# Expert weights through one ring of ten 2 MB pieces, and late blocks ahead of the expert's own up-projection

## The chip, the cores and the metric

One Trainium2 chip (trn2), one core of it. The time is that of the whole program on the device in microseconds (us); lower is better. All arithmetic is in float32.

## What is computed

One inference step of a hybrid decoder layer for 320 tokens (256 of a prompt, 64 of a sample group). The front of the layer (RMSNorm, an input projection, a convolution branch, a gated delta rule and a merge) is not touched by the change. What matters is the mixture of experts behind it:

```python
N_EXPERTS = 32; TOP_K = 4; D_MODEL = D_FF = 1024
logits = (h @ router_w) + router_b                    # 320 tokens
top_logit, top_idx = lax.top_k(logits, TOP_K)
gate = softmax(top_logit)
# for every expert e and the tokens that chose it:
gu = xe @ w_gate_up[e] + b_gate_up[e]                 # 1024 x 2048
gt, up = split(gu)
act = (clip(up, -7, 7) + 1) * (min(gt, 7) * sigmoid(1.702 * gt))
y = act @ w_down[e] + b_down[e]                       # 1024 x 1024
x = x + sum over the 4 experts of gate * y
```

The weights of one expert are 8 MB (gate and up) and 4 MB (down), 12 MB in all, and all 32 experts are read from HBM.

## The kernel before

The experts are computed one after the other. Each expert has 64 slots for its tokens (`SLOTS`). A token beyond the 64th goes into a **late block** of 32 slots (`LATE`); there can be up to 8 of them for an expert (`LATER`), and a table `flags` in SBUF, computed at run time from the routing, says which are needed. Every engine reads it with `value_load` and branches with `If`. In the data used here two of the 32 experts (numbers 10 and 30) need one late block each: the groups of the trace on 32 slots have twice the count of one block, and the two places are visible in time.

**The weights.** SBUF holds two buffers of 8 MB (`gu[0]`, `gu[1]`) for gate and up, used by even and odd experts in turn, and one buffer of 4 MB (`dn`) for the down weights. SyncE (SP) loads them in 2 MB transfers, four for a `gu` and two for a `dn`, each with its own semaphore. `released(e)` waits until the last down matmul of expert e is done (`y_mm`, and `late_y_mm` where the expert has late blocks), and then SP issues six transfers in a row: `dn` for expert e+1 and `gu` for expert e+2.

**TensorE (PE)**, in this order for each expert e: `up` (the bias, line 1007, then 32 matmuls against `gu`, line 1012), `gather` of the tokens of expert e+1 (line 986), for even e the `combine` of the pair before (line 1030), `turn_x` (line 994), the transposes of the activation (line 1088), `down` (16 matmuls against `dn`, line 1023). Most matmuls of the loop are 64 columns wide and go in pairs to two halves of the array. Where an expert has a late block, `late_up` is run ahead of the expert's own `down`, and `late_down` behind it, so that VectorE and ScalarE work on the late activation (`clamp`, the sigmoid, `swiglu`) while PE runs its own `down`. A further loop, `Fori(1, LATER)`, is entered only if a second late block is flagged.

**VectorE (DVE)** places the tokens of the next expert (line 1471), clamps and multiplies (lines 1495 to 1503), and adds the results to the residual (line 1510). **ScalarE (ACT)** does the sigmoid and the copies out of PSUM (lines 602 to 615).

PE, DVE, ACT and SP each run their own loop of 16 turns, two experts a turn, tied together by semaphores only. The code of both late variants (the straight one and the one in `Fori`) lies in the loop body, and is jumped over where it isn't needed.

Of the kernel before, what the change touches and what calls it, by code (L numbers as in the profile page):

```python
# [25 lines left out]
E = 32  # L26
SLOTS = 64
# [76 lines left out]
def hybrid_step(nc, xT, x_prompt, x_sample, w_main, w_ab, params, consts, conv_state, short_state,  # L104
# [3 lines left out]
    with ExitStack() as ctx:  # L108
# [91 lines left out]
        f[0] = gu_at[0] + 6 * 2 * D  # L200
# [54 lines left out]
        fg = region(KD * 2 * D, D)  # L255
        yout = region(KD * 2 * D + D, NT, D)
# [38 lines left out]
        def _(sp):  # L295
# [38 lines left out]
            def load_gu(e, p, parts=range(KD // 2)):  # L334
                for r in parts:
                    sp.dma_start(gu[p][:, 2 * r:2 * r + 2], w_gate_up[bass.ds(e, 1), 2 * r * P:2 * (r + 1) * P, :]
                                 .rearrange("o (k p) n -> p (o k) n", p=P)).then_inc(sem(f"ld_gu{p}_{r}"), 16)

            def load_dn(e):
                for r in range(2):  # L340
                    sp.dma_start(dn[:, 4 * r:4 * r + 4], w_down[bass.ds(e, 1), 4 * r * P:4 * (r + 1) * P, :]
                                 .rearrange("o (k p) n -> p (o k) n", p=P)).then_inc(sem(f"ld_dn{r}"), 16)


# [4 lines left out]
            load_gu(0, 0, (0, 1, 2))  # L349
# [3 lines left out]
            load_dn(0)  # L353
            load_gu(1, 1, (1,))
# [5 lines left out]
            load_gu(1, 1, (0,))  # L360

            sp.wait_ge(sem(FRONT_STORES[-1][0]), FRONT_STORES[-1][1])
            load_gu(0, 0, (3,))
# [3 lines left out]
            load_gu(1, 1, (2, 3))  # L367
            blocks = sp.alloc_register("sp_blocks")
            sp.reg_mov(blocks, 0)

            def released(e):

                sp.wait_ge(sem("y_mm"), e + 1)
                later = sp.value_load(flags[0:1, bass.ds(e * LATER, 1)], min_val=0, max_val=1)
                with sp.If(later):
                    sp.reg_add(blocks, blocks, 1)
                    more = sp.value_load(flags[0:1, bass.ds(e * LATER + 1, 1)], min_val=0, max_val=1)
                    with sp.If(more):
                        with sp.Fori(1, LATER) as b:
                            f = sp.value_load(flags[0:1, bass.ds(e * LATER + b, 1)], min_val=0, max_val=1)  # L380
                            with sp.If(f):
                                sp.reg_add(blocks, blocks, 1)
# [57 lines left out]
        def _(act):  # L440
# [157 lines left out]
            with expert_loop(act, 0, E // 2) as i:  # L598
                for p in range(2):
                    e = 2 * i + p  # L600
                    act.wait_ge(sem("clamped"), e + 1)
                    act.activation(actb, tmp, ACT.Sigmoid, scale=ALPHA).then_inc(sem("sig"), 1)  # L602
                    act.wait_ge(sem("x_gathered"), e + 2)
                    act.wait_ge(sem("xg_mm"), e + 1)
                    act.activation(xt, ps[:, 3, :], ACT.Copy).then_inc(sem("xt_ready"), 1)  # L605
                    act.wait_ge(sem("t_mm"), e + 1)
                    act.activation(actT, heads(0, P, P), ACT.Copy).then_inc(sem("gt_ready"), 1)  # L607
                    if p:
                        act.activation(gT, ps[:, 1, 0:N], ACT.Copy).then_inc(sem("gt_ready"), 1)  # L609
                    later = act.value_load(flags[0:1, bass.ds(e * LATER, 1)], min_val=0, max_val=1)  # L610
                    with act.If(later):
                        late_up(act.snap(blocks))
                    act.wait_ge(sem("y_mm"), e + 1)
                    act.activation(ysb[SLOTS * p:SLOTS * (p + 1), 0], ps[0:SLOTS, 2, :], ACT.Copy)  # L614
                    act.activation(ysb[SLOTS * p:SLOTS * (p + 1), 1], ps[SLOTS:P, 2, :],
                                   ACT.Copy).then_inc(sem("y_ready"), 1)
                    with act.If(later):
                        late_down(act.snap(blocks))
                        act.reg_add(blocks, blocks, 1)
                        more = act.value_load(flags[0:1, bass.ds(e * LATER + 1, 1)], min_val=0, max_val=1)  # L620
                        with act.If(more):
                            with act.Fori(1, LATER) as b:
                                f = act.value_load(flags[0:1, bass.ds(e * LATER + b, 1)], min_val=0, max_val=1)
                                with act.If(f):
                                    m = act.snap(blocks)
                                    late_up(m)
                                    late_down(m)
                                    act.reg_add(blocks, blocks, 1)
# [9 lines left out]
        def _(pe):  # L638
# [365 lines left out]
            def up(slots, outs, tokens, s, w, waits, done):  # L1004
# [3 lines left out]
                for k in range(KD):  # L1008
                    if waits is not None and k % 2 == 0:
                        pe.wait_ge(waits[k // 2][0], waits[k // 2][1])  # L1010
                    for q in range(4):
                        m = pe.matmul(outs[q], tokens[:, k % 4, k // 4], w[:, k, q * 512:(q + 1) * 512],  # L1012
                                      start=False, stop=(k == KD - 1))
                m.then_inc(done, 1)

            def down(slots, arrived, ready, done, i):
                pe.wait_ge(ready, i)
                for k in range(KD):
                    if arrived is not None and k % 4 == 0:
                        pe.wait_ge(sem(f"ld_dn{k // 4}"), arrived)  # L1020
                    for c in range(2):
                        a = (k // 4) * slots
                        m = pe.matmul(ps[slots * c:slots * (c + 1), 2, :], actT[:, k % 4, a:a + slots],  # L1023
                                      dn[:, k, c * 512:(c + 1) * 512], start=(k == 0), stop=(k == KD - 1))
                m.then_inc(done, 1)
# [46 lines left out]
            with expert_loop(pe, 0, E // 2) as i:  # L1072
                for p in range(2):
# [13 lines left out]
                    for j in range(4):  # L1087
                        m = pe.transpose(ps[:, 0, j * P:(j + 1) * P], actb[:, j * P:(j + 1) * P], ident)  # L1088
# [573 lines left out]
```

## Time and profile before

| what | value |
|---|---|
| time, median of 3 runs | 1512.07 us (1510.52 to 1519.53) |
| time of the profiled execution | 1514.72 us |
| its span, first to last instruction | 1512.9 us |
| mean granted TensorE clock | 0.956 of full speed |
| PE busy | 1408.2 us (93%) |
| DVE busy, ACT busy | 490.8 us (32%), 216.8 us (14%) |
| moved by DMA | 444.70 MB, mean 294 GB/s |

The first 457 us are the front of the layer, then the expert loop runs to about 1496 us, then comes the end (two norms and the store). Matmuls are pipelined, so their durations overlap: the time that a series takes is read from its first start to the start of what follows. Granted clock 1.00 is 2.4 GHz, and 0.5 is 1.2 GHz.

### The profile page before, as it was taken

The page shows a single profiled execution, that of the slowest core. Times are in us where ns is not written, and L with a number is a line of the kernel's source. Part 1 is how long each engine was busy: PE and PEld are TensorE (multiplying, and loading weights), DVE is VectorE, ACT ScalarE, POOL GpSimd, SP SyncE. Part 2 cuts the span into 40 slices and gives each one's busy share as a digit, 9 for nine tenths or more (in the row PEclk, how much of TensorE's full clock was granted, in tenths as well). Part 3 has the DMA queues.
Part 4 walks back from the last instruction along what each step waited for, and adds up shares of the span by engine and source line. Part 5 has one row for each costly group of instructions (what it writes and reads, how often), then busy time and mean ns, then how long its engine had stood idle before and what let it go on. Part 6 is the DMA issues. An engine that isn't in the chain of part 4 may idle for free.

```text
span 1512.9 us, 17366 instructions
## 1 busy us (share of the span) xinstructions
PE 1408.2 (93%) x6338; PEld 661.5 (44%) x6339; DVE 490.8 (32%) x1237; ACT 216.8 (14%) x364; POOL 36.5 (2%) x44
## 2 busy tenths in 40 slices
PE   6997998998979899999999999999999999999996
PEld 4665766886433333333333333333333333333332
DVE  2596626433453122221322132122221222213223
ACT  2111252210110101111110111101111011111102
POOL 3101001000000000000000000000000000000000
PEclk9998998987968999999998999999999999999999
DMA  9748212014382999999993899999999999999941
GB/s 245 141 134 85 92 56 56 1 57 138 158 340 113 387 396 420 418 416 417 419 419 121 353 402 419 415 401 419 409 417 396 409 416 408 417 417 419 418 159 35
DMA packets 82924, 444.70 MB, mean 294 GB/s; under 512 B 6224, under 2 KB 7136, under 8 KB 50000
## 3 DMA queue, kind: packets, MB, share of 16 engines
q1 hardware_dynamic: 79600, 435.88, 74.2%
q0 software_dynamic: 2720, 7.13, 1.9%
q10 hardware_dynamic: 576, 1.31, 0.3%
q8 instruction: 18, 0.29, 0.1%
q14 instruction: 10, 0.08, 0.0%
HBM read 439.92 MB, written 4.39 MB: 294 GB/s over the span
## 4 chain that ended last, share of the span: by engine, by line
PE 90%; DMA 4%; DVE 2%; ACT 2%; issue 1%; ACTq 0%; DVEq 0%; SPq 0%
PE ps L1012 30%; PE ps L1023 16%; PE ps L669 9%; PE ps L986 7%; PE ps L1030 6%; PE ps L1007 4%; DMA arena<-in_w_main 2%; PE ps L887 2%; DMA arena<-in_b_gate_up 1%; PE ps L880 1%; PE ps L774 1%; PE ps L708 1%; PE ps L994 1%; PE ps L653 1%; PE ps L1088 1%
## 5 line engine op out<-in xcount | busy, mean ns | idle before, releaser
L1012 PE MATMUL ps<-arena 128*64 128x512 f32 (+1 forms) x2176 | 472.0, 595 | 0.0
L1012 PEld LDWEIGHTS ps<-arena 128*64 128x64 f32 (+1 forms) x2176 | 168.4, 136 | 290.7 <-issue 290.7
L1023 PE MATMUL ps<-arena 128*64 128x512 f32 (+1 forms) x1088 | 260.0, 611 | 19.1 <-ACT arena L609 17.5
L1495 DVE TENSOR_SCALAR arena<-ps 128x512 f32<-128x512 f32 (+1 forms) x34 | 23.6, 693 | 674.1 <-PE ps L1012 674.1
L669 PE MATMUL ps<-arena 128*128 128x320 f32 x576 | 162.0, 445 | 16.5 <-DMA arena<-in_w_main 10.9
L1023 PEld LDWEIGHTS ps<-arena 128*64 128x64 f32 (+1 forms) x1088 | 85.4, 139 | 167.9 <-issue 166.0
L669 PEld LDWEIGHTS ps<-arena 128*128 128x128 f32 x576 | 112.5, 196 | 65.6 <-issue 20.2
L986 PE MATMUL ps<-arena 128*64 128x512 f32 (+3 forms) x420 | 115.9, 617 | 8.9 <-DMA arena<-in_b_gate_up 5.0
L1030 PE MATMUL ps<-arena 128*128 128x512 f32 (+3 forms) x228 | 101.9, 606 | 3.8 <-ACT arena L592 1.4
L1510 DVE TENSOR_TENSOR arena<-arena,ps 128x512 f32<-128x512 f32 (+1 forms) x114 | 72.7, 680 | 61.8 <-PE ps L1030 61.8
L602 ACT ACTIVATE arena<-arena 128x512 f32<-128x512 f32 x32 | 20.2, 632 | 483.6 <-DVE arena L1495 483.6
L1007 PE MATMUL ps<-arena 128*64 128x512 f32 (+1 forms) x272 | 78.0, 633 | 3.7 <-issue 2.4
L986 PEld LDWEIGHTS ps<-arena 128*64 128x64 f32 (+3 forms) x420 | 30.4, 135 | 78.0 <-issue 72.4
L1030 PEld LDWEIGHTS ps<-arena 128*128 128x128 f32 (+3 forms) x228 | 34.1, 171 | 60.0 <-issue 53.3
L1182 DVE SCALAR_TENSOR_TENSOR arena<-arena 128x256 f32<-128x256 f32 x120 | 56.7, 472 | 0.0
L614 ACT ACTIVATE arena<-ps 64x512 f32<-64x512 f32 x32 | 18.9, 591 | 249.5 <-PE ps L1023 249.5
L1007 PEld LDWEIGHTS ps<-arena 128*64 128x64 f32 (+1 forms) x272 | 22.5, 139 | 41.9 <-issue 40.4
L1490 DVE TENSOR_TENSOR arena<-ps,arena 128x256 f32<-128x256 f32 (+1 forms) x70 | 26.0, 413 | 45.3 <-PE ps L994 33.3
L1185 DVE SCALAR_TENSOR_TENSOR arena<-arena 128x64 f32<-128x64 f32 x120 | 32.7, 272 | 0.0
L607 ACT ACTIVATE arena<-ps 128x512 f32<-128x512 f32 x32 | 19.2, 600 | 88.1 <-PE ps L1088 62.4
L994 PE MATMUL ps<-arena 128*128 128x128 f32 x132 | 21.2, 285 | 11.2 <-ACT arena L605 11.2
L1477 DVE TENSOR_SCALAR arena<-arena 128x64 f32<-128x64 f32 (+3 forms) x108 | 30.4, 311 | 1.3
(280 smaller groups left out, 1008.3 us busy)
## 6 DMA issues: line engine op xcount, KB each, us to landing
arena<-in_w_gate_up SPq DMA_DIRECT2D x128, 2048.0 KB, 24.1
arena<-in_w_down SPq DMA_DIRECT2D x64, 2048.0 KB, 12.4
arena<-in_w_main SPq DMA_DIRECT2D x40, 512.0 KB, 3.7
arena<-in_w_merge_out SPq DMA_DIRECT2D x1, 3072.0 KB, 10.2
arena<-in_w_conv_out POOLq DMA_DIRECT2D x1, 2048.0 KB, 14.2
arena<-in_w_delta_out SPq DMA_DIRECT2D x1, 2048.0 KB, 8.0
out_delta_s<-arena POOLq DMA_DIRECT2D x1, 2048.0 KB, 20.7
arena<-in_xT SPq DMA_DIRECT2D x1, 1280.0 KB, 6.4
```

The costliest lines, as they stand in the source:

```text
L669: i = pe.matmul(ps[:, j, 0:N], wring[:, j, k], hT[:, k], start=(k == 0), stop=(k == KD - 1))
L887: i = pe.matmul(ps[0:P, 2 * t + c, :], mixed[:, k, tok(t)], wm[k][:, c * 512:(c + 1) * 512], start=(k == 0), stop=(k == KD - 1))
L986: m = pe.matmul(ps[slots * c:slots * (c + 1), 3, :], pk[rows(t), t, 0:slots], h2_of(t)[:, c * 512:(c + 1) * 512], start=(t == 0), stop=(t ...
L994: return pe.transpose(out, rows_in, ident)
L1007: pe.matmul(outs[q], s[:, q, 0:slots], bg, start=True, stop=False)
L1012: m = pe.matmul(outs[q], tokens[:, k % 4, k // 4], w[:, k, q * 512:(q + 1) * 512], start=False, stop=(k == KD - 1))
L1023: m = pe.matmul(ps[slots * c:slots * (c + 1), 2, :], actT[:, k % 4, a:a + slots], dn[:, k, c * 512:(c + 1) * 512], start=(k == 0), stop=(k ...
L1030: m = pe.matmul(ps[0:TILES[t][1], COMBINE_BANKS[t][c], :], g(c)[:, tok(t)], y(c), start=True, stop=True)
L1182: stt(out=cacc[:, j, 0:NP], in0=cext[:, j, bass.ds(w, NP)], scalar=dw_w[:, j, bass.ds(w, 1)], in1=cacc[:, j, 0:NP], op0=ALU.mult, op1=ALU. ...
L1185: stt(out=seqs(cacc[:, j]), in0=cext_s[:, j, :, bass.ds(w, TS)], scalar=dw_w[:, j, bass.ds(w, 1)], in1=seqs(cacc[:, j]), op0=ALU.mult, op1 ...
L1477: i = ts(out(t), iot(rows(t)), pos[rows(t), t, bass.ds(e, 1)], gates[rows(t), t, bass.ds(e, 1)], ALU.is_equal, ALU.mult)
L1510: tt(part, part, ps[0:n, COMBINE_BANKS[t][c], :], ALU.add).then_inc(done, 1)
```

## The change

**The ring.** The same 20 MB of SBUF are cut into ten slots of 2 MB. An expert's weights are six pieces (four of gate and up, two of down), numbered through all experts; piece n goes into slot n mod 10. A new semaphore `used` counts pieces whose last matmul is done; SP waits for it before each piece, and each refill is one transfer, instead of six behind one wait. `released` and SP's reading of `flags` are gone.

**The loops.** Since six pieces and ten slots repeat only after five experts, and the parity of two experts is needed too, the loop bodies of PE, DVE and ACT now hold ten experts (`BODY`), three turns, and the last two experts are written out behind the loop. SP's loop holds thirty pieces, five turns.

**Late blocks.** `late_up` and `late_down` are joined to `late_block`, which runs at the head of the expert, ahead of its own `up`. All late blocks go through one `Fori(0, LATER)` with an `If` inside; it is entered if the first flag is set, and makes 8 turns. The flag of a second block is no longer asked for before the loop. DVE and ACT do the same in their own loops.

```diff
+BODY = 10
+RING_SLOTS, PER_EXPERT = 10, 6
+SLOT_AT = [16384, 20480, 24576, 28672, 32768, 36864, 4096, 0, 8192, 12288]
...
-        gu_at = [KD * 2 * D, 0]
-        gu = [region(at_, KD, 2 * D) for at_ in gu_at]
-        dn = region(2 * KD * 2 * D, KD, D)
+        gu_slot = [region(a, 2, 2 * D) for a in SLOT_AT]
+        dn_slot = [region(a, 4, D) for a in SLOT_AT]
...
+            def load(e, u, slot):
+
+                if u < 4:
+                    rows_in = w_gate_up[bass.ds(e, 1), 2 * u * P:2 * (u + 1) * P, :]
+                    out = gu_slot[slot]
+                else:
+                    rows_in = w_down[bass.ds(e, 1), 4 * (u - 4) * P:4 * (u - 3) * P, :]
+                    out = dn_slot[slot]
+                sp.dma_start(out, rows_in.rearrange("o (k p) n -> p (o k) n", p=P)).then_inc(sem(f"ld_ring{slot}"), 16)
...
-            load_gu(1, 1, (2, 3))
...
-            def released(e):
-
-                sp.wait_ge(sem("y_mm"), e + 1)
-                later = sp.value_load(flags[0:1, bass.ds(e * LATER, 1)], min_val=0, max_val=1)
-                with sp.If(later):
-                    sp.reg_add(blocks, blocks, 1)
...
-                    sp.wait_ge(sem("late_y_mm"), sp.snap(blocks))
-                    sp.sem_inc(sem("late_released"), 1)
...
-            with expert_loop(sp, 0, E // 2 - 1) as i:
-                for p in range(2):
-                    released(2 * i + p)
-                    load_dn(2 * i + (p + 1))
-                    load_gu(2 * i + (p + 2), p)
-            released(E - 2)
-            load_dn(E - 1)
+            load(1, 2, 8)
+            load(1, 3, 9)
...
+            def refill(first, n):
+
+                u = n % PER_EXPERT
+                sp.wait_ge(sem("used"), first * PER_EXPERT + (n + 1 - RING_SLOTS))
+                load(first + n // PER_EXPERT, u, n % RING_SLOTS)
+
+            for n in range(RING_SLOTS, 5 * PER_EXPERT):
+                refill(0, n)
+            with expert_loop(sp, 1, E // 5) as i:
+                for n in range(5 * PER_EXPERT):
+                    refill(5 * i, n)
+            for n in range(2 * PER_EXPERT):
+                refill(E - 2, n)
+            sp.wait_ge(sem("used"), (E - 2) * PER_EXPERT + 3)
...
+                act.wait_ge(sem("used"), PER_EXPERT * e + 6)
...
+            def arrived(laps, n, u):
+
+                g = n * PER_EXPERT + u
+                pe.wait_ge(sem(f"ld_ring{g % RING_SLOTS}"), laps + 16 * (g // RING_SLOTS + 1))
+                return g % RING_SLOTS
...
+                for u in range(4):
+                    w = gu_slot[arrived(laps, n, u)]
+                    for r in range(2):
+                        k = 2 * u + r
+                        for q in range(4):
+                            m = pe.matmul(outs[q], tokens[:, k % 4, k // 4], w[:, r, q * 512:(q + 1) * 512],
+                                          start=False, stop=(k == KD - 1))
+                    if slots == SLOTS:
+                        m.then_inc(sem("used"), 1)
+                    elif u == 3:
+                        m.then_inc(done, 1)
...
+                for u in range(4, 6):
+                    w = dn_slot[arrived(laps, n, u)]
...
+                    if slots == SLOTS:
+                        m.then_inc(sem("used"), 1)
...
+            def late_block(m, laps, n):
...
+                up(LATE, [ps[LATE * q:LATE * (q + 1), 0, :] for q in range(4)], late_xg, sel[n % 2],
+                   laps, n, sem("late_h_mm"))
...
+                down(LATE, laps, n, sem("late_gt_ready"), sem("late_y_mm"), m + 1)
...
-            with expert_loop(pe, 0, E // 2) as i:
-                for p in range(2):
...
-                    later = pe.value_load(flags[0:1, bass.ds(e * LATER, 1)], min_val=0, max_val=1)
-                    with pe.If(later):
-
-                        pe.wait_ge(sem("gt_ready"), down_ready)
-                        late_up(pe.snap(blocks), p)
-                    down(SLOTS, 16 * e + 16, sem("gt_ready"), sem("y_mm"), down_ready)
-                    with pe.If(later):
-                        late_down(pe.snap(blocks))
-                        pe.reg_add(blocks, blocks, 1)
-                        more = pe.value_load(flags[0:1, bass.ds(e * LATER + 1, 1)], min_val=0, max_val=1)
-                        with pe.If(more):
-                            with pe.Fori(1, LATER) as b:
-                                f = pe.value_load(flags[0:1, bass.ds(e * LATER + b, 1)], min_val=0, max_val=1)
-                                with pe.If(f):
-                                    m = pe.snap(blocks)
-                                    late_up(m, p)
-                                    late_down(m)
-                                    pe.reg_add(blocks, blocks, 1)
+            def expert(first, pairs, laps, n):
+
+                e, p, pair = first + n, n % 2, pairs + n // 2
+                pe.wait_ge(sem("xg_ready"), e + 1)
+                pe.wait_ge(sem("sel_ready"), e + 1)
+                later = pe.value_load(flags[0:1, bass.ds(e * LATER, 1)], min_val=0, max_val=1)
+                with pe.If(later):
+                    with pe.Fori(0, LATER) as b:
+                        f = pe.value_load(flags[0:1, bass.ds(e * LATER + b, 1)], min_val=0, max_val=1)
+                        with pe.If(f):
+                            late_block(pe.snap(blocks), laps, n)
+                            pe.reg_add(blocks, blocks, 1)
+                up(SLOTS, [ps[SLOTS * (q % 2):SLOTS * (q % 2 + 1), q // 2, :] for q in range(4)], xg[p], sel[p],
+                   laps, n, None)
+                gather(SLOTS, sem("p_ready"), sem("x_gathered"), e + 2)
...
+                down(SLOTS, laps, n, sem("gt_ready"), None, 3 * pair + (3 if p else 1))
+
+            with expert_loop(pe, 0, E // BODY) as i:
+                for n in range(BODY):
+                    expert(BODY * i, BODY // 2 * i, 16 * PER_EXPERT * BODY // RING_SLOTS * i, n)
+            for n in range(E % BODY):
+                first = E - E % BODY
+                expert(first, first // 2, 16 * PER_EXPERT * first // RING_SLOTS, n)
...
+            def clamp(n, gate, mm, count, clamped):
+                dve.wait_ge(mm, count)
```

**PE, the place of the late block.** Before, in the body for an even expert: behind the last combine (line 1030), the flag is read, and the late gather, turn and up (on 32 slots) stand ahead of `down` (line 1023).

```order
L1030 MATMUL ps<-arena 64x512 x2
L1099 ISA
L1099 TENSOR_LOAD arena
L1099 ISA x2
L1100 COMPARE_AND_BRANCH
L1102 ISA
L1103 ISA
L986 MATMUL ps<-arena 32x512 x6
L995 MATMUL ps<-arena 128x64 x4
L1007 MATMUL ps<-arena 32x512 x4
L1012 MATMUL ps<-arena 32x512 x32
```

Now, at the end of the late block (late down, line 1028, and combine, line 1038) and the head of the expert's own up (lines 1007 and 1013):

```order
L1028 MATMUL ps<-arena 32x512 x16
L1038 MATMUL ps<-arena 128x512 x4
L1062 ISA
L1038 MATMUL ps<-arena 64x512 x2
L1088 REGISTER_ALU
L1086 UNCONDITIONAL_BRANCH
L1084 REGISTER_ALU
L1084 COMPARE_AND_BRANCH
L1083 UNCONDITIONAL_BRANCH
L1007 MATMUL ps<-arena 64x512 x4
L1001 ISA
L1013 MATMUL ps<-arena 64x512 x32
```

The late block has moved from around the expert's own `down` to ahead of its own `up`, and the counter and back branch of the loop over late blocks (line 1084) stand between the two.

**PE, the head of the late block.** What is passed on the way from the flag to the first late matmul, for every expert; both COMPARE_AND_BRANCH rows can jump, the first over the whole block (lines 1083 to 1088), the second over one turn of it:

```order
L1082 ISA
L1082 TENSOR_LOAD arena
L1082 ISA x2
L1083 COMPARE_AND_BRANCH
L1084 UNCONDITIONAL_BRANCH
L1084 ISA
L1085 TENSOR_LOAD arena
L1085 ISA x2
L1086 COMPARE_AND_BRANCH
L1087 ISA
L980 MATMUL ps<-arena 32x512 x6
```

Each turn of the loop over late blocks, also one without a block, passes lines 1085, 1086 and 1084.

**SP, the refills.** Before, six transfers stand in a row behind one wait (lines 341 and 336; the row on line 374 belongs to the wait for the next expert):

```order
L341 DMA arena<-in_w_down 128x4x1024
L336 ISA
L336 DMA arena<-in_w_gate_up 128x2x2048
L336 ISA
L336 DMA arena<-in_w_gate_up 128x2x2048
L336 ISA
L336 DMA arena<-in_w_gate_up 128x2x2048
L336 ISA
L336 DMA arena<-in_w_gate_up 128x2x2048
L374 ISA
```

Now each transfer has its own wait (line 376, with a register), and there is no flag to read:

```order
L376 REGISTER_ALU
L344 ISA
L344 DMA arena<-in_w_down 128x4x1024
L376 REGISTER_ALU
L344 ISA
L344 DMA arena<-in_w_down 128x4x1024
L376 REGISTER_ALU
L344 ISA
L344 DMA arena<-in_w_gate_up 128x2x2048
```

## Rows read from the trace of the kernel before

**Rows 1.** The page, busy time by engine, and DMA in 40 slices.

```profile
PE 1408.2 (93%) x6338; PEld 661.5 (44%) x6339; DVE 490.8 (32%) x1237; ACT 216.8 (14%) x364; POOL 36.5 (2%) x44
...
DMA  9748212014382999999993899999999999999941
```

**Rows 2.** Windows: stretch, length, busy PE, PEld, DVE, ACT, POOL, clock, DMA, GB/s.

```profile
641.80:701.80 60.00, 58.21 (x267) 21.98 (x263) 14.23 (x32) 7.64 (x12) 0.00 (x0) 1.00 1.02 418
761.80:827.00 65.20, 59.82 (x285) 19.72 (x283) 16.41 (x35) 8.00 (x13) 0.00 (x0) 0.92 0.61 246
917.00:978.70 61.70, 59.91 (x265) 22.43 (x263) 14.24 (x32) 7.64 (x12) 0.00 (x0) 0.97 1.02 417
1163.40:1224.90 61.50, 59.71 (x267) 22.05 (x263) 14.24 (x32) 7.64 (x12) 0.00 (x0) 0.97 1.01 408
1404.80:1465.00 60.20, 54.97 (x285) 18.48 (x279) 15.58 (x34) 8.00 (x13) 0.00 (x0) 1.00 0.65 262
```

**Rows 3.** Waits, 457 to 1505 us: who waited for whom, us, times, longest.

```profile
PE ps L1023 <- ACT arena L609: 17.5, 16, 1.1
...
PE ps L994 <- ACT arena L605: 11.2, 16, 0.7
...
PE ps L986 <- DVE arena L1471: 3.9, 2, 1.9
```

**Rows 4.** DMA issues, 641 to 702 us: count, size, median us to landing.

```profile
arena<-in_w_gate_up SPq DMA_DIRECT2D x8, 2048.0 KB, 24.9
```

**Rows 5.** Chain of waits, whole loop: start, us, what (gathers at experts 8 to 11).

```profile
717.25 2.72 PE ps L986 x12
...
748.66 2.75 PE ps L986 x11
...
777.23 2.72 PE ps L986 x12
...
843.89 2.75 PE ps L986 x12
```

**Rows 6.** Chain of waits, 1404 to 1500 us: expert 30 with its late block.

```profile
1420.27 2.72 PE ps L986 x12
...
1431.31 2.92 PE ps L986 x12
...
1444.51 7.02 PE ps L1023 x32
1451.53 1.03 PE ps L995 x8
...
1465.34 1.94 PE ps L1007 x8
...
1481.01 2.75 PE ps L986 x12
```

**Rows 7.** Timeline of DVE, 1444 to 1448 us: the activation of that late block.

```profile
1444.58 0.68 DVE L1495 TENSOR_SCALAR arena<-ps 64x512 f32<-64x512 f32 x1 [6.42 <-PE ps L1012]
...
1447.40 0.68 DVE L1503 SCALAR_TENSOR_TENSOR arena<-arena 64x512 f32<-64x512 f32 x1
```

**Rows 8.** Sources of L1108, L1100 and L1105: PE's sequencer, ns min/median/max, starts.

```profile
L1108 PEldq TENSOR_LOAD <-arena x2: 312/314/315, 825.4 to 1464.3; - x2
...
L1100 PEldq COMPARE_BRANCH  x32: 83/223/340, 481.9 to 1485.6; - x32
...
L1105 PEldq COMPARE_BRANCH  x32: 67/227/5888, 486.4 to 1489.7; - x32
...
L1105 PEldq COMPARE_BRANCH  x2: 670/3279/5888, 486.4 to 515.0; - x2
```

**Rows 9.** Timeline of PE at 521 us, the first back edge.

```profile
521.64 0.65 PE L1007 MATMUL ps<-arena 128*64 128x512 f32 x2 [2.23 <-issue]
```

**Rows 10.** DMA queues, 457 to 522 us, then 522 to 1480 us: packets, MB, share.

```profile
q8 instruction: 6, 0.10, 0.6%
...
q1 hardware_dynamic: 63522, 370.70, 94.9%
```

More of the change, by code:

```diff
@@ L198, in hybrid_step @@
         unit = early(P)
-        f[0] = gu_at[0] + 6 * 2 * D
+        f[0] = SLOT_AT[3]
         s0 = early(NSEQ * H, P)
@@ L630, in _ @@
+            with expert_loop(act, 0, E // BODY) as i:
+                for n in range(BODY):
+                    expert(BODY * i, n)
+            for n in range(E % BODY):
+                expert(E - E % BODY, n)
             for t in range(NT):
@@ L1002, in turn_x, with up @@
                 m.then_inc(done, 1)
-            def up(slots, outs, tokens, s, w, waits, done):
+            def arrived(laps, n, u):
+                g = n * PER_EXPERT + u
+                pe.wait_ge(sem(f"ld_ring{g % RING_SLOTS}"), laps + 16 * (g // RING_SLOTS + 1))
+                return g % RING_SLOTS
+            def up(slots, outs, tokens, s, laps, n, done):
                 for q in range(4):
                     pe.matmul(outs[q], s[:, q, 0:slots], bg, start=True, stop=False)
[L1008 to L1014, printed above, removed]
@@ new lines, in down @@
+            def down(slots, laps, n, ready, done, i):
+                pe.wait_ge(ready, i)
+                for u in range(4, 6):
+                    w = dn_slot[arrived(laps, n, u)]
+                    for r in range(4):
+                        k = 4 * (u - 4) + r
+                        for c in range(2):
+                            a = (k // 4) * slots
+                            m = pe.matmul(ps[slots * c:slots * (c + 1), 2, :], actT[:, k % 4, a:a + slots],
+                                          w[:, r, c * 512:(c + 1) * 512], start=(k == 0), stop=(k == KD - 1))
+                    if slots == SLOTS:
+                        m.then_inc(sem("used"), 1)
+                    elif u == 5:
+                        m.then_inc(done, 1)
@@ L1122, in _ @@
+            combine(1, *halves, sem("c_mm"))
             pe.wait_ge(sem("added"), 3 * E + 2)
-            combine(2, *pair, sem("c_mm"))
+            combine(2, *halves, sem("c_mm"))
         @block.vector
@@ new lines, in expert @@
+            def expert(first, pairs, n):
+                e, p, pair = first + n, n % 2, pairs + n // 2
+                dve.wait_ge(sem("x_gathered"), e + 1)
+                later = dve.value_load(flags[0:1, bass.ds(e * LATER, 1)], min_val=0, max_val=1)
+                with dve.If(later):
+                    with dve.Fori(0, LATER) as b:
+                        f = dve.value_load(flags[0:1, bass.ds(e * LATER + b, 1)], min_val=0, max_val=1)
+                        with dve.If(f):
+                            late_block(e, lambda r: iota[r, bass.ds(b * LATE + SLOTS, LATE)], dve.snap(blocks))
+                            dve.reg_add(blocks, blocks, 1)
+                place(e + 1, first_slots, SLOTS, sem("p_ready"))
+                select(e + 1, 1 - p)
+                clamp(P, ps[:, 0, :], sem("used"), PER_EXPERT * e + 4, sem("clamped"))
+                weigh(e, lambda t: pg[rows(t), t, p], first_slots)
+                swiglu(P, ps[:, 1, :], sem("sig"), sem("act_ready"), sem("swiglu_step"), e)
+                if p == 0:
+                    add(0, sem("c_mm"), sem("added"), pair)
+                move_x(xg[1 - p], SLOTS, sem("xg_mm"), sem("xg_ready"), e + 2)
+                if p == 0:
+                    add(1, sem("c_mm"), sem("added"), pair)
+                    add(2, sem("c_mm"), sem("added"), pair)
@@ L1577, in final_norm @@
+            with expert_loop(dve, 0, E // BODY) as i:
+                for n in range(BODY):
+                    expert(BODY * i, BODY // 2 * i, n)
+            for n in range(E % BODY):
+                expert(E - E % BODY, (E - E % BODY) // 2, n)
             def final_norm(t):
```

190 lines of the change are left out of this document (60 added, 130 removed).

## The prediction

> **What bounds the kernel now.** I read the page first, for the engines; then windows of two experts each; then the list of waits; and the chain of waits for what stands between two gathers. PE is busy 93% of the span, and in the expert loop nearly always; but the DMA engines are full there too [rows 1]. So which of them sets the pace? An undisturbed pair of experts takes 60.0 us, 58.2 of them PE busy at full clock, while DMA moves at 418 GB/s [rows 2]. A pair's weights are 12 pieces of 2 MB (2.097 million bytes), 25.17 MB, which at 418 GB/s take 60.2 us. The two are level, within 0.2 us a pair. The list of waits decides: over the whole loop PE waits for ACT (17.5 and 11.2 us in 16 times, the small gaps of every odd expert) and for DVE ahead of a late block [rows 3]. No row of that list has PE or its weight loads waiting for a DMA. The weights are just in time (24.9 us from issue to landing, behind a queue of other pieces [rows 4]), but in time. The loop is bound by PE, and what is not paid for by PE's own matmuls is: the small ACT gaps, two late blocks, five pairs at a granted clock of 0.97 (from 917 to 1225 us, 61.5 to 61.7 us each; first and last in [rows 2]), and one stall of 2.2 us [rows 9].
>
> **The ring (refills piece by piece).** It removes SP's wait for the whole expert: the first refill can start when the first two k-rows of expert 0 are done, where before it had to wait for that expert's down; by the windows of an expert that is some 25 us earlier. It doesn't change bytes or the number of transfers (192 of 2 MB), so the DMA pace stays 60.2 us a pair. A PE that never waited for DMA can't gain from earlier pieces: worth 0. It costs 0 as well: the pieces are ahead by some 25 us at the start and lose 0.2 us a pair, 3 us in 16 pairs. The longest stretch without a release, a late block, finds the ring full behind it. In the two late pairs DMA share falls to 0.61 and 0.65 [rows 2], so DMA has slack there before and after. The waits per piece on PE are as many as before (six an expert), increments ride on matmuls, and SP's register adds lie in a queue that otherwise waits. If that cover were gone (a piece late by 1 us in each expert) it would be 32 us; nothing in the rows asks for it.
>
> **The late blocks.** First their price before. Gathers of consecutive experts stand 748.66 - 717.25 = 31.4 us apart from even to odd; with the late block of expert 10 it is 843.89 - 777.23 = 66.7 [rows 5], and with that of expert 30 it is 1481.01 - 1420.27 = 60.7 [rows 6]. So they cost 35.2 and 29.3 us. The 5.9 between them go with the clock: 0.92 in the first stretch, 1.00 in the second [rows 2].
> Now the same work ahead of the expert's own up, from the second. (a) Gather, turn and up: 1444.51 - 1431.31 = 13.2 us. The wait of 1.9 us for DVE ahead of them [rows 3] goes, since DVE has the tokens placed long before; it is not counted in the 13.2. (b) Then PE needs the activation. Before, the expert's own down (7.0 us, 1444.51 to 1451.53 [rows 6]) covered that; now nothing does. DVE starts 1444.58 and ends 1447.40 + 0.68 = 1448.08 [rows 7]: 3.6 us idle PE. (c) The turns, the late down and the combine: 1465.34 - 1451.53 = 13.8 us. Together 30.6 us.
> (d) The loop over late blocks now makes eight turns, seven of them empty. Each reads a flag and passes two branches and a register add. The row for it: the one check of a second block before, whose load starts at 1464.3 [rows 8], is over when up starts at 1465.34 [rows 6], so 1.0 us for load, assertion and branch; another branch is 0.22 [rows 8], with the add and the gaps of a load's neighbours I take 0.4 more. 1.4 x 7 = 9.8 us a late expert; bounds 1.0 x 7 = 7 and 1.6 x 7 = 11. PE has only the last combine queued, 1.1 us, to cover it, so 8.7 are seen. DVE and ACT make the same empty turns at the same time, not longer ones, and have the next clamp 14 us later.
> Sum: 30.6 + 8.7 = 39.3 us for a late expert against 29.3: +10.0 each. For expert 10 I let the clock cost what it cost before. For expert 30, PE now pauses 3.6 and 8.7 us where it paused not at all and the granted clock may fall: between 0 and the 5.9 that expert 10 shows; I take 3. **+23 us** for the late blocks.
>
> **The longer body.** Every expert without a late block (30) jumps over it once, about 310 instructions; and there are two back edges and a fall out of the loop. Before there were two such jumps an expert, of some 190 and 430, and sixteen turns. (A float32 matmul is two MATMULs and two weight loads in the trace; counted so in the listings, a body had some 1,770 instructions on PE before, and has some 5,800 now.) Of the jumps the trace shows: the branch on line 1105 takes 0.23 us as a rule, and once 5.9 us, in the first turn [rows 8]. PE stood still for 2.23 us after it [rows 9]. PE's queue thus covers 3.7 us of a slow branch. In that first turn 6 packets came on the instruction queue, and none from 522 to 1480 us [rows 10]: a body that has been loaded is run without loading. The body of ten experts is new in its first turn and, if what was loaded is only kept for a body of the old size, new in the other two as well. Bounds: 0 (loading goes on ahead, and jumps stay cheap, as both on line 1100 and one of two on line 1105 were in the first turn, 0.67 us at most [rows 8]), and 32 x 2.23 = 71 us (each jump and back edge like the slow one). The jump is nearer to the short one in length, and of the long ones one in two was cheap; I take three to four slow ones, at the back edges and where a jump lands far out, 4 x 2.23 = 8.9, less the one of before: **+7 us**.
> The Trainium skill speaks against this part of the change: "Runtime: NRT & Kernel Launch", section on instruction fetch, says that TensorE holds 2048 instructions, refilled in blocks of 256, that straight code is loaded ahead, and that a taken branch to a target outside what is held waits for a load. By its figures the old body fits and the new one doesn't (an estimate from that page), so it would have every turn of the new body load again; whether each jump then stalls is the rival below.
>
> **The clock.** The five pairs at 0.97 cost 1.5 to 1.7 us each, 8 in all. Where PE's gaps fall decides it, and these shift: between -8 and +8, and I take 0.
>
> **Sum.** The profiled execution took 1514.7 us, 2.6 over the median of the runs. 1514.7 + 23 + 7 = 1544.7, and on the scale of the median 1542.
>
> **Rivals.**
> *Code loading at each jump.* If each of the 30 jumps and 2 back edges is like the slow one, 1512 + 23 + 71 = 1606 us. For it: the page's rule, and that jumps over loaded code are the only ones that the steady state shows. Against: three of four jumps in the first turn were under 0.7 us. From 3.7 us on a branch is seen on PE at all, so single short loads would cost nothing. Chance 0.25, for all from ten slow jumps on (1560 and more).
> *No change.* The clock gives it back: PE's phase shifts, the five pairs run at 60.0 (-8), expert 10 escapes its half clock (-5.9), expert 30 keeps its full clock (-3), and no jump is slow (-7): 1542 - 24 = 1518 us. The point: granted clock 1.00 in all pairs. For it: 0.97 in only five of sixteen pairs, so it is a matter of phase. Against: PE now has longer pauses. Chance 0.17 for 1497 to 1527.
> *The ring is worth something.* If PE were paced by the weights after all, in ways that the list of waits doesn't tell, the slow pairs (8), the stall of 2.2 and the 5.9 of expert 10 could be such time, and go, with the late blocks' new gaps hidden in it: 1512 - 16 = 1496 us. For it: DMA at 418 GB/s as full as PE. Against: no wait for a DMA in the list, and the time lost lies where the granted clock is low. Chance 0.03.
> *The forecast,* 1527 to 1560: 0.55.
>
> **Range and chances.** About 1% (15 us) is what a measurement can tell from no change. The lower end reaches to the no-change case, 1519; the upper takes in the code loading up to 24 slow jumps, 1512 + 23 + 54 = 1589. Faster by over 1%: 0.03; within 1%: 0.17; slower: 0.80.
>
> **What would show it.** In the chain of waits after: pairs still 60.0 us; at experts 10 and 30 a PE gap of 3.6 us ahead of the late transposes, and one of 8 to 10 ahead of L1007, with no late wait for DVE; gather to gather 71 and 71 us in place of 66.7 and 60.7. Instruction packets on q8 all through the loop, some 70 more. The branch on line 1083 short in most experts, over 3.7 us in three or four. Refills landing well ahead of use. The forecast is wrong if the pair itself isn't 60.0, if that branch is long in most experts, or if the empty turns of the late loop cost much less or more than 1.4 us.

## The result and the profile after

The changed kernel takes 1563.11 us (median of 4 runs, 1559.92 to 1569.85), the kernel before 1515.36 us beside it: ratio **1.032 [1.029, 1.035]**. The profiled execution of after has a span of 1568.1 us, 55.2 more than before; it is the longest of the four runs (1569.85), so the rows show some 7 us more than the medians do.

The page: PE busy, the instruction queue, and the first matmuls of `up` with PE's idle time ahead of them.

```profile
PE 1430.1 (91%) x6338; PEld 660.2 (42%) x6339; DVE 491.8 (31%) x1237; ACT 202.8 (13%) x353; POOL 36.6 (2%) x44
...
q8 instruction: 86, 1.41, 0.4%
...
L1007 PE MATMUL ps<-arena 128*64 128x512 f32 (+1 forms) x272 | 87.7, 688 | 35.2 <-issue 34.0
```

As many matmuls as before (x6338), with 22 us more of busy time, and 34 us marked "issue": idle time of PE in which it waited for nothing that the profile shows.

Waits from 457 to 1565 us, and DMA issues from 457 to 1500 us.

```profile
PE ps L1007 <- issue: 34.0, 10, 9.3
...
PE ps L1028 <- ACT arena L612: 16.5, 16, 1.1
...
PE ps L988 <- ACT arena L608: 11.2, 16, 0.7
...
PE ps L989 <- DVE arena L1504: 7.3, 2, 3.6
```

```profile
arena<-in_w_gate_up SPq DMA_DIRECT2D x122, 2048.0 KB, 13.0
```

The small ACT gaps are those of [rows 3], the first of them 1 us less in all (16.5 for 17.5). The wait for DVE's place is gone, and the uncovered activation (L989 for L1504) has come, 3.6 us twice. The pieces land 13.0 us after their issue, where [rows 4] had 24.9 (24.5 over the whole loop): a single refill has fewer others ahead of it than one of six issued together. No row has PE waiting for a DMA, before or after.

The chain of waits from 757 to 880 us, expert 10 with its late block at the head (start, us, what).

```profile
757.96 2.75 PE ps L980 x11
...
778.45 1.94 PE ps L1007 x8
780.38 8.85 PE ps L1013 x64
...
795.23 10.03 PE ps L1028 x32
...
809.52 9.32 issue
818.84 3.33 PE ps L1007 x8
822.16 13.73 PE ps L1013 x64
835.89 2.72 PE ps L980 x12
```

Gather to gather (L980) is 835.89 - 757.96 = 77.9 us, and at expert 30 it is 77.9 again, where I had 71. The row of 9.32 us is the seven empty turns; VectorE stands 10.1 us in its own at the same time, and ScalarE 8.8. The late up takes 1.94 + 8.85 us and the late down 10.03. In the chain of before that [rows 6] is taken from, the same three are:

```profile
1436.58 1.07 PE ps L1007 x8
1437.64 6.87 PE ps L1012 x64
...
1453.86 7.08 PE ps L1023 x32
```

The windows of after tell why (stretch, length, busy PE, PEld, DVE, ACT, POOL, clock, DMA, GB/s):

```profile
777.30:784.10 6.80, 6.22 (x32) 1.76 (x34) 2.02 (x8) 0.50 (x1) 0.00 (x0) 0.50 0.64 266
784.10:794.40 10.30, 6.65 (x59) 2.41 (x51) 2.75 (x4) 0.63 (x1) 0.00 (x0) 1.00 0.01 2
794.40:801.20 6.80, 6.01 (x15) 1.30 (x16) 0.00 (x0) 0.70 (x2) 0.00 (x0) 0.50 0.00 0
801.20:811.40 10.20, 7.09 (x32) 1.78 (x28) 3.74 (x6) 0.59 (x1) 0.00 (x0) 1.00 0.00 0
811.40:821.70 10.30, 2.86 (x8) 1.05 (x10) 0.72 (x4) 1.28 (x1) 0.00 (x0) 0.50 0.00 0
```

The granted clock is 0.50 (1.2 GHz) in three stretches around the late block: 23.9 us. Around the same block before it was one of 10.2 and one of 3.4, and at expert 30 none. Each fall comes after a pause of PE: ahead of the late transposes of the tokens (1.2 us), of the activation (3.6 us), and in the empty turns. A fourth stretch of 3.4 us lies between the same two gathers, at 763.6 us, behind the small gap of 1.0 us ahead of the odd expert's down, and expert 30 has one too; before, the late pairs had none there. From 784 us on the DMA share is 0: all ten slots are full.

The branch on line 1083 over the late block (PE's sequencer; ns min/median/max), then its slowest, and a stall after a short one with PE's timeline.

```profile
L1083 PEldq COMPARE_BRANCH  x32: 71/360/6132, 457.9 to 1517.1; - x32
...
L1083 PEldq COMPARE_BRANCH  x1: 6132/6132/6132, 1312.1 to 1312.1; - x1
...
L1083 PEldq COMPARE_BRANCH  x1: 355/355/355, 876.9 to 876.9; - x1
```

```profile
880.25 0.59 PE L1007 MATMUL ps<-arena 128*64 128x512 f32 x1
883.11 1.12 PE L1007 MATMUL ps<-arena 128*64 128x512 f32 x2 [2.28 <-issue]
```

The branch is short in most experts and over 3.7 us in four (4.7 to 6.1); six more took 1.5 to 1.9 us, with no stall behind them. The chain shows 2.56, 1.35, 1.96 and 2.62 us of idle PE behind those four. It shows 2.18, 2.28 and 2.13 more behind branches of 0.35 us: at 883 us one matmul behind the jump ran, and the next came late. All stalls but the empty turns are 34.0 - 9.32 - 9.13 = 15.6 us, where before had 2.2.

**Where the 55.2 us are.** The time from DVE's clamp of one expert to that of the next (both experts of a pair) splits the loop. An undisturbed pair has 59.9 to 60.0 us in both kernels. The two pairs with late blocks took 184.5 us together before and 218.7 after: **+34.2**. The rest of the loop took 19.4 more: 13.4 of stalls, and eight pairs with a stretch of half clock instead of five, 1.6 us each, 4.8; 1.2 aren't placed. Three of the eight stretches begin in or within 1.1 us of a stall (those at 521, 645 and 881 us), the other five behind the small gap as before. Whether the stalls made them isn't shown: the kernel of old buffers and one turn below has no stall in its loop and eight such stretches too. The front took 1.7 more.

### The profile page after: what moved, and what is told of

Same layout as the page of the kernel before. It is cut to its first block, busy times and chain, and to the rows that moved or that the text cites. A ratio compares the mean times of both kernels' runs of the same rounds, so it can differ in the third digit from the quotient of the medians.

```text
span 1568.1 us, 17347 instructions
## 1 busy us (share of the span) xinstructions
PE 1430.1 (91%) x6338; PEld 660.2 (42%) x6339; DVE 491.8 (31%) x1237; ACT 202.8 (13%) x353; POOL 36.6 (2%) x44
## 4 chain that ended last, share of the span: by engine, by line
PE 89%; DMA 3%; issue 3%; DVE 2%; ACT 2%; ACTq 0%; DVEq 0%; SPq 0%
PE ps L1013 29%; PE ps L1028 16%; PE ps L663 9%; PE ps L980 6%; PE ps L1038 6%; PE ps L1007 4%; PE ps L881 2%; DMA arena<-in_w_main 2%; DMA arena<-in_b_gate_up 1%; PE ps L874 1%; PE ps L768 1%; PE ps L702 1%; PE ps L988 1%; PE ps L647 1%; PE ps L1100 1%
## 5 line engine op out<-in xcount | busy, mean ns | idle before, releaser
L1013 PE MATMUL ps<-arena 128*64 128x512 f32 (+1 forms) x2176 | 479.3, 602 | 0.0
L1028 PE MATMUL ps<-arena 128*64 128x512 f32 (+1 forms) x1088 | 270.5, 628 | 18.1 <-ACT arena L612 16.5
L980 PE MATMUL ps<-arena 128*64 128x512 f32 (+3 forms) x420 | 117.7, 609 | 5.3 <-DMA arena<-in_b_gate_up 5.3
L1007 PE MATMUL ps<-arena 128*64 128x512 f32 (+1 forms) x272 | 87.7, 688 | 35.2 <-issue 34.0
L980 PEld LDWEIGHTS ps<-arena 128*64 128x64 f32 (+3 forms) x420 | 30.7, 135 | 75.4 <-issue 75.4
L1007 PEld LDWEIGHTS ps<-arena 128*64 128x64 f32 (+1 forms) x272 | 23.2, 148 | 77.5 <-issue 76.0
L1472 DVE TENSOR_SCALAR arena<-arena 128x64 f32<-128x64 f32 (+3 forms) x105 | 23.5, 254 | 36.5 <-issue 35.3
L1478 DVE TENSOR_SCALAR arena<-arena 128x64 f32<-128x64 f32 (+3 forms) x108 | 30.4, 311 | 1.3
## 6 DMA issues: line engine op xcount, KB each, us to landing
arena<-in_w_conv_out POOLq DMA_DIRECT2D x1, 2048.0 KB, 13.4
```

The costliest lines, as they stand in the source:

```text
L980: m = pe.matmul(ps[slots * c:slots * (c + 1), 3, :], pk[rows(t), t, 0:slots], h2_of(t)[:, c * 512:(c + 1) * 512], start=(t == 0), stop=(t ...
L1013: m = pe.matmul(outs[q], tokens[:, k % 4, k // 4], w[:, r, q * 512:(q + 1) * 512], start=False, stop=(k == KD - 1))
L1478: i = ts(out(t), iot(rows(t)), pos[rows(t), t, bass.ds(e, 1)], gates[rows(t), t, bass.ds(e, 1)], ALU.is_equal, ALU.mult)
```

## The experiments

Ratios are to runs of the kernel before on the same chip, with 95% intervals. Each says whether it has the ring or the old buffers (two of 8 MB, one of 4 MB, and SP's wait for a whole expert).

**One turn.** In the changed kernel, on PE, ACT and DVE:

```diff
-                    with pe.Fori(0, LATER) as b:
+                    with pe.Fori(0, 1) as b:
```

> The changed kernel with a loop over late blocks of one turn instead of eight, on PE, DVE and ACT; later late blocks, which the data doesn't need, are left out. Changed kernel 1563. Theory (seven empty turns stand between late block and own up, 9.3 and 9.1 us of PE idle 'issue' ahead of L1007): both gaps fall below 1 us, so 17 us less, and up to 6 us more where the granted clock then falls less: 1541, within 1535 to 1547. Rival (PE waits there for something else, the late adds of DVE or code that is loaded): no change, 1560 to 1563.

1542.3 us, 1.0153 [1.0099, 1.0207]. The waits (457 to 1540 us):

```profile
PE ps L1007 <- issue: 12.2, 8, 2.7
```

The two waits of over 9 us are gone, and with them 21 us by the medians and 25 by the ratios: 18.4 of gaps, the rest half clock and stalls (12.2 us for 15.6). In the profiled runs the two late pairs take 191.8 us together, 26.9 less: 8.5 us beyond the gaps. The price of the empty turns held: 9.2 us seen, and the last combine's 1.1 beside it, over 7 is 1.5 us a turn.

**Order alone, with old buffers and bodies of two.** The kernel before with `late_block` at the head of each expert, eight turns:

```diff
+BODY = 2
...
+            def late_block(m, e, n, waits):
...
+                up(LATE, [ps[LATE * q:LATE * (q + 1), 0, :] for q in range(4)], late_xg, sel[n % 2],
+                   gu[n % 2], waits, sem("late_h_mm"))
...
+                down(LATE, 16 * e + 16, sem("late_gt_ready"), sem("late_y_mm"), m + 1)
```

> The kernel before (its two gu buffers and one dn, SP unchanged, body of two experts) with the late block ahead of the expert's own up and the loop of eight turns, as in the change. Before 1515. Theory (late order and empty turns cost some 30 of the 48 us, long body the rest, ring nothing): 1545, within 1540 to 1552, no instruction packets from the third expert on, L1007 waiting for issue only at the two late experts and once at the first back edge. Rival (the ring or the long body costs nearly all): 1517 to 1525.

1549.58 us, 1.019 [1.0153, 1.0228]. Waits from 457 to 1550 us:

```profile
PE ps L1008 <- issue: 19.1, 3, 9.3
```

The late pairs take 109.4 and 107.8 us, where the changed kernel has 109.3 twice, and beside the two gaps of 9.3 there is one stall of 0.5 us. So 32.7 of the +34.2 come with order and turns alone, without the ring and without the longer body; the 1.5 between them is one stretch of half clock more or less.

**The same with one turn** (`Fori(0, 1)`):

> As e2_ahead_body2 (old buffers, body of two experts, late block ahead of the own up), with one turn in the late loop in place of eight. Before 1518. Theory (the new place of the late block costs only the uncovered activation, 3.6 us against 1.9 before, and lower clock in two places): 1523 to 1528; the late experts as in e1_one_turn, some 36 us each. Rival (the place itself costs most of the 31 us of e2_ahead_body2): over 1540.

1524.31 us, 1.0065 [1.0042, 1.0087]: the order alone costs 10 us (6 to 13 by the interval), the seven empty turns of two experts 19, by the two ratios. By the late pairs it is 10.9 and 21.8. The late pairs took 98.5 and 96.9 us, 10.9 more than before. For this part the prediction had 5.6 (2 x 1.3, and 3 of clock). Half clock in them is 30.7 us, where before had 13.7; 17 us at half speed is some 8.5 lost, and 10.9 - 8.5 = 2.4 is the 2 x 1.3 of the sum.

**The same as the second, with bodies of ten** (old buffers):

```diff
-BODY = 2
+BODY = 10
```

> As e2_ahead_body2, but PE, DVE and ACT with bodies of ten experts and the last two written out; SP and buffers as before. Theory (code loading on the long body costs 13 us, the ring nothing): 1558 to 1563, the same as the changed kernel, with some 70 instruction packets in the loop and about eight stalls of 2 to 2.6 us. Rival (the ring itself costs the rest, by single waits and later issue): as e2_ahead_body2, 1545. Third (old buffers miss the weights when code packets come between): over 1570, with PE waiting for weights.

1576.68 us, 1.0353 [1.0307, 1.04]. The waits:

```profile
PE ps L1008 <- issue: 36.3, 10, 9.3
```

The instruction queue shows 86 packets, against 16 with bodies of two: the stalls come with the long body, and need no ring. But 13.6 us over the changed kernel (5 us by the two ratios, each to its own runs of the kernel before) is more than I had expected. Is that a gain of the ring, or spread? Both were run again side by side, in five rounds.

> The changed kernel once more, beside the same order and bodies of ten with the old buffers and SP's old waits, on one chip. Both theories expect 1.032 of the kernel before (1.029 to 1.035), as in its own comparison; it is there so that the other has a neighbour on the same chip.

> Late blocks ahead, eight turns, bodies of ten, but the two buffers of gate and up and SP's wait for a whole expert as before. My theory (the ring is worth nothing while the PE is slower than the weights): the same ratio as the changed kernel beside it, within 0.3%, both 1.032 to 1.034. Rival (the ring gains what the first comparison of the two showed, 1.0353 against 1.0318): 0.3 to 0.5% above the changed kernel, 5 to 8 us, and then the records must show a wait or a slower pair in this kernel that the changed one doesn't have.

The changed kernel 1563.15 us, 1.0309 [1.0283, 1.0335]; with old buffers 1566.06 us, 1.0349 [1.0316, 1.0382]. Their waits, ring first:

```profile
PE ps L1007 <- issue: 31.6, 10, 9.3
```

```profile
PE ps L1008 <- issue: 35.3, 10, 9.3
```

The medians are 2.9 us apart, and the ratios by 0.4%, which is what the rival expected; the loops differ by 4.0 us from first to last clamp, and waits for a DMA are in neither. The intervals overlap, and the profiled spans are 0.8 us apart. Two differences of rows repeat. PE's wait for ACT ahead of the down of odd experts is 16.5 us in 16 times with the ring and 17.4 or 17.5 without, 1 us in the whole loop. And the stalls, less the two waits of over 9 us, are 15.6 and then 13.0 us with the ring, 17.8 and then 16.8 without. Whether the ring shortens these stalls, or the other kernel's code only lies otherwise, no run tells; so what the ring gains above that one us in this pair of kernels stays open.

**No late code at all**, in the changed kernel and in the kernel before: the value loads, branches and late blocks are taken out of PE, ACT, DVE (and of SP), so the tokens beyond the 64th of two experts are left out.

> The changed kernel without any late code on PE, DVE and ACT, so the tokens beyond slot 64 of two experts are left out. The body of ten experts is then some 2,650 instructions on PE, with no jump but the back edges. Theory (loading costs only where a jump leaves what is loaded): instruction packets go on through the loop, but PE waits for issue at most at the back edges; every pair 60.0 us but for the granted clock, time 1438 to 1446, within 6 us of e7_before_no_late. Rival (a long body costs by its length, 0.4 us an expert): 13 us over e7_before_no_late.

> The kernel before without late code on PE, DVE, ACT and SP, so the same tokens are left out. Theory: late blocks cost 29 and 35 us, so 1518 - 64 = 1454, less what the clock gives back (8): 1440 to 1454, no PE wait for weights though nothing lets them catch up now (0.25 us lost a pair, 4 us in all). Rival (the weights were only in time because of the late blocks): PE waits for a DMA in the last pairs.

1449.08 us, 0.9578 [0.9543, 0.9613], and 1451.56 us, 0.9585 [0.9552, 0.9619]. The page of each, ring first:

```profile
q8 instruction: 47, 0.77, 0.2%
```

```profile
q8 instruction: 14, 0.23, 0.1%
```

The ring's body of ten is still loaded anew in every turn (47 packets), and costs nothing: no wait of PE on issue is left in the list. This agrees with the Trainium skill, "Runtime: NRT & Kernel Launch", section "Instruction fetch mechanics", by which straight code is loaded ahead. In the changed kernel every stall stands at the first matmuls behind the jump over the late block (L1007), so the jump over code that isn't needed is the likely cost. But the straight body is also less than half as long (some 2,650 instructions for 5,800), and jump and amount of code were not varied apart. The kernel with the ring came out 3 us over my range, with seven stretches of half clock between first and last clamp. The ring is worth next to nothing here: the two are 2.5 us apart with intervals that overlap, and a pair at full clock takes 59.9 us with it and 60.0 without.

**The small gap of odd experts.** If PE is what bounds, a shorter gap must shorten the pair. In the kernel before, the down of an odd expert waits for the transposed activation alone, and no longer for the transposed gates:

```diff
-                    down_ready = 3 * i + (3 if p else 1)
+                    down_ready = 3 * i + (2 if p else 1)
...
+                    if p:
+                        pe.wait_ge(sem("gt_ready"), 3 * i + 3)
```

> The kernel before, with one wait moved: in odd experts the own down waits for the copy of the activation only, and the copy of the gates (L609) is waited for behind the down. Before 1515. Theory (PE sets the pace): the gap of 1.1 us ahead of L1023 in 16 experts shrinks by 0.45 to 0.6 us, 7 to 10 us less: 1506 to 1508. Rival (DMA is level with PE at 60.2 us a pair, so a PE pair of 59.4 runs into the weights after some five pairs): 1511 to 1515, with PE waits for a DMA that the kernel before doesn't have.

1514.76 us, 0.9966 [0.9943, 0.999]. The row that had 17.5 us in [rows 3] is now:

```profile
PE ps L1023 <- ACT arena L607: 12.3, 16, 0.8
```

The gap fell by 0.33 us and the pair with it, 59.98 to 59.65. Less than I had expected, since ACT still began only when the transposes of the gates were done. So those got an increment of their own:

```diff
-                    act.wait_ge(sem("t_mm"), e + 1)
+                    act.wait_ge(sem("t_mm"), 3 * i + p + 1)
...
+                        act.wait_ge(sem("t_mm"), 3 * i + 3)
```

> As e4_early_down, and in odd experts the transposes of the activation are told to ACT before those of the gates, so that its copy starts 0.33 us earlier and PE's gate transposes lie beside it. Theory (PE sets the pace, the gap ahead of L1023 falls from 0.77 to some 0.45 us in 16 experts): a pair of 59.3 us, 5 us under e4_early_down, ratio to before 0.993. Rival (the weights at 60.2 us a pair set the pace from here): no further gain, PE waits for weights.

1499.51 us, **0.991 [0.9877, 0.9943]**: faster than both kernels, than the one before by about 1%. Its windows, an early and a late pair, and its waits:

```profile
600.00:659.20 59.20, 58.16 (x264) 21.95 (x263) 14.20 (x33) 7.62 (x13) 0.00 (x0) 1.00 1.02 418
...
1180.00:1240.24 60.24, 58.41 (x265) 21.80 (x263) 14.23 (x32) 7.66 (x13) 0.00 (x0) 1.00 1.02 418
```

```profile
PE ps L995 <- ACT arena L605: 11.2, 16, 0.7
PE ps L1024 <- ACT arena L607: 5.5, 16, 0.3
PE ps L1013 <- DMA arena<-in_w_gate_up: 3.9, 5, 0.8
```

Pairs of 59.23 us at first, and 60.24 from expert 20 on, at full clock, with PE waiting for weights: that is 25.17 MB at 418 GB/s. Here is the other bound, 0.26 us above the pair of before: that kernel lived on the lead of its weights, and PE set its pace.

**Is the ring worth something beyond it?** The same two edits without late code (the same tokens left out), with the ring and with the old buffers:

> The changed kernel without the code of late blocks (it leaves out the tokens beyond the 64th of two experts), and with the order that shortened the PE's pair to 59.24 us: own down waits for the transposed activation alone, the transposed gates come behind it. Is the ring worth something once the PE is quicker than the weights (60.2 us a pair)? Theory: yes. Its first refill starts some 25 us earlier, a pair at 59.24 loses 1.0 us of that lead, so in 16 pairs it is never used up: all pairs 59.2, no wait for a DMA, 1449 - 12 = 1437 us, ratio 0.950, and some 10 us less than the same with the old buffers beside it. Rival (nothing, since both keep the DMA queue full): the same time as its neighbour within 3 us, near 1450.

> The same two steps (no late code, so the same tokens left out; gates behind the down) with the old buffers and SP's wait for the whole expert. Where the late code was kept, pairs were 59.24 us at first and 60.24 from expert 20 on, after the late block of expert 10 had given the transfers time to catch up; the lead of the old buffers was thus some 5 us. Theory: used up by expert 10, then 60.24 us for some 11 pairs and short PE waits for gate and up DMAs: 1450 us, ratio 0.957 to 0.959. Rival (the ring and the old buffers alike): no wait for a DMA or the same waits in both, the two within 3 us.

1428.26 us, 0.9426 [0.9396, 0.9457], and 1431.99 us, 0.9442 [0.941, 0.9474]. Windows of the ring, then the windows and waits of the old buffers:

```profile
1180.00:1239.16 59.16, 58.20 (x265) 21.70 (x263) 14.11 (x32) 6.36 (x11) 0.00 (x0) 1.00 1.02 417
```

```profile
1180.00:1240.24 60.24, 58.40 (x266) 21.81 (x263) 14.11 (x32) 7.64 (x12) 0.00 (x0) 1.00 1.02 418
```

```profile
PEld ps L985 <- DMA arena<-in_w_gate_up: 15.4, 16, 1.7
PE ps L985 <- DMA arena<-in_w_gate_up: 6.0, 8, 0.8
```

The mechanism is there: with the ring all pairs take 59.1 to 59.2 us and no wait for a DMA is in the list; with the old buffers they are 60.24 from expert 18 on, with the waits shown. The old lead lasted longer than I had said (expert 16, not 10). Between first and last clamp the two are 8.7 us apart in the traces, which is eight pairs at 1.1 us; by the medians they are 3.7 apart, and the intervals overlap: the direction is shown by the rows, the size is not settled (the profiled run is the fastest of its four with the ring and the slowest of its four without). By the same reckoning the ring's larger lead is spent too, 1.1 us a pair at 417 GB/s, and would run out in a longer loop; that is an estimate, no run shows it. The two came out 9 and 18 us faster than expected, in part for a reason that I hadn't counted: with no pause of PE over 0.7 us neither trace has a stretch of half clock between these clamps, where the two kernels without late code but with the gap of 1.1 us had seven and six.

## Why the prediction was right, and where its sizes were off

- **Direction, bound, ring.** PE bounds the loop, the pair stayed at 60.0 us, and the ring moved nothing: held, by the two kernels without late code and by the wait that appears only when PE is made 0.75 us a pair faster. "Worth 0" is true of this PE, and not of a faster one, and with the long body the old buffers were 0.4% slower, which stays open.
- **Late blocks, +23.** The steps held one by one: the wait for DVE's place went, the activation stood bare for 3.6 us, twice, the empty turns were 9.3 and 9.1 us for my 8.7. Mis-sized was the clock's term in it, "between 0 and the 5.9 that expert 10 shows; I take 3", and nothing for expert 10. The rest of the measured +34.2, after 2.6 for the steps and 18.4 for the turns, is 13.2 us: both experts now run three stretches at half clock around the block, and one of 3.4 us ahead of it. Expert 30 has 9.6 of it, over my upper bound of 5.9 (2.8 in the late up, 2.9 in the late down, 1.5 in the first matmuls of its own up, 1.6 in the stretch ahead, the rest not placed), and expert 10 has 3.5, where I had let it keep its old clock although PE pauses twice more there than it did.
- **Code loading, +7.** The four slow jumps came as forecast, with 8.5 us for my 8.9. Missed were the stalls behind short branches, 6.6 us in three and 0.5 in one more: 13.4 in place of 7. The row that I sized by (the branch's own duration) can't show them, and that my count of slow jumps came out to the number is partly luck: the bounds were 0 and 71 us. The rival that puts a stall at every jump is excluded: at least 22 of the 30 jumps passed without one. Packets rose by 68 for my 70.
- **The clock elsewhere, 0.** It was +4.8, three more pairs with a half-clock stretch, within my 8 either way; what set their number wasn't found. The rival of no change needed a clock of 1.00 in all pairs; it fell lower instead.
- **The sum.** +30 forecast in the profiled execution, +55 measured: 11 from the late blocks, 6 from stalls, 5 from the clock, the rest front and unplaced. By the medians it is 48 us. Of the 25 that I missed, 15 are the granted clock: 10 in the late experts, 5 in other pairs.
- **The range.** 1563 us lies inside 1519 to 1589, but 3 us above the 1527 to 1560 that I gave the forecast itself (0.55), and in the band that I gave to code loading at ten jumps or more (0.25). That mechanism didn't come: eight stalls cost 15.6 us. The range held because its upper end was stretched for slow jumps, and the granted clock filled that room; so the time was met partly by luck, while direction and steps were met by reasoning.

## What to carry to other kernels

A pause of the TensorE costs more than its length where the granted clock falls behind it, as around the late blocks here (7 us beside the pauses at expert 30): when an edit adds pauses of some us, price the matmuls around each of them at half clock, and take no disturbed place as already paid for. A loop with a flag inside costs every turn on each engine, 1.3 to 1.5 us here, also where it finds nothing to do. Two bounds within half a per cent of each other (59.98 and 60.24 us a pair) hide each other's remedies: the ring could show its worth only after the PE's gap was cut.

## What the runs showed that I had not expected

- Instruction loads alone cost nothing: 47 packets in straight bodies of ten, no stall; 86 packets with one jump of some 310 instructions an expert, 12 to 18 us of stalls in three kernels and two repeats. The straight body has less than half the code, so the jump is only the likely cause. Some stalls come behind a branch that itself took 0.35 us, one matmul later. The back edges of the long body were cheap (0.34 us).
- The half-clock stretches outside the late experts went altogether where PE's longest gap in a pair fell to 0.7 us (three kernels), and were still there at 0.8 and 1.1. Each had cost 1.5 to 1.7 us. These are rows of the kernels here, not a limit that was searched for.
- Early transfers end as a DMA share of 0.00: with all ten slots full there is nothing to move until the expert's own up frees a slot.
